# Reordering the second norm of a decoder layer: residual add, sums of squares, modulation groups and a larger ring of conditioning loads

## What is computed

```python
mod = jax.nn.silu(c) @ ada_w[l] + ada_b[l]
sh1, sc1, g1, sh2, sc2, g2 = jnp.split(mod[:, None, :], 6, axis=-1)
h = rms_norm(x) * (1.0 + sc1) + sh1
mix, ... = token_mixer(h, ...)          # ends with  merged @ w_out
x = x + g1 * mix
h = rms_norm(x) * (1.0 + sc2) + sh2
ff, s_cv = conv_ffn(h, ...)             # begins with  h @ w_up
x = x + g2 * ff
```

## Time and profile before

| what | value |
|---|---|
| three runs | 2243.47, 2246.07, 2248.70 us |
| median | 2246.07 us |
| profiled execution: span | 2245.0 us; its own time beside the span is not listed apart from the three runs |
| TensorE busy | 2200.8 us, 98% of the span |
| VectorE, ScalarE, GpSimd busy | 50%, 44%, 15% |
| DMA | 460.03 MB, mean 205 GB/s |
| granted TensorE clock, mean | 0.993 |

### The profile page before, as it was taken

How to read it: one execution, slowest core, us unless ns; L and a number is a source line. 1 busy time by engine, 2 the same in 40 slices (tenths; PEclk the granted TensorE clock), 3 DMA queues, 4 the chain that set the end, 5 groups by cost and what they waited for, 6 DMA issues and landing times. The chain is left out here.

```text
span 2245.0 us, 42389 instructions
## 1 busy us (share of the span) xinstructions
PE 2200.8 (98%) x17346; PEld 2073.4 (92%) x17346; DVE 1123.0 (50%) x1557; ACT 985.4 (44%) x1365; POOL 342.1 (15%) x529
## 2 busy tenths in 40 slices
PE   7999999999999999999999998999999999999998
PEld 3689999999999999999999987999999999999997
DVE  3346465564565444444445565555555555444443
ACT  3336463564454344454435334434434344333332
POOL 2000312322222221121202241000000000010000
PEclk9999999999999999999999999999999999999999
DMA  9987666666666767668666688555555555555553
GB/s 350 376 279 213 195 198 203 205 199 211 205 212 205 221 188 224 214 205 254 211 209 209 209 284 282 160 168 167 160 168 159 168 168 159 177 161 174 171 167 106
DMA packets 407411, 460.03 MB, mean 205 GB/s; under 512 B 14843, under 2 KB 379955, under 8 KB 406433
## 3 DMA queue, kind: packets, MB, share of 16 engines
q1 hardware_dynamic: 394192, 410.64, 57.2%
q0 software_dynamic: 12240, 46.03, 6.6%
q10 hardware_dynamic: 833, 1.26, 0.2%
HBM read 431.48 MB, written 26.39 MB: 204 GB/s over the span
## 5 line engine op out<-in xcount | busy, mean ns | idle before, releaser
L763 PE MATMUL ps<-xh,whi 128*128 128x288 f32 x3968 | 1195.1, 301 | 11.4 <-DVE xl L1745 5.0
L1688 DVE TENSOR_TENSOR wlo<-raw,whi 128x1024 fp32r<-128x1024 f32 x584 | 735.3, 1260 | 918.3 <-ACT whi L1255 916.0
L765 PE MATMUL ps<-xh,wlo 128*128 128x288 f32 x3968 | 1173.1, 296 | 0.0
L764 PE MATMUL ps<-xl,whi 128*128 128x288 f32 x3968 | 1172.0, 295 | 0.0
L1255 ACT ACTIVATE whi<-raw 128x1024 fp32r<-128x1024 f32 x584 | 616.6, 1057 | 764.5 <-PE ps L765 728.4
L763 PEld LDWEIGHTS ps<-xh,whi 128*128 128x128 f32 x3968 | 748.2, 189 | 53.4 <-issue 38.7
L764 PEld LDWEIGHTS ps<-xl,whi 128*128 128x128 f32 x3968 | 747.5, 188 | 0.0
L765 PEld LDWEIGHTS ps<-xh,wlo 128*128 128x128 f32 x3968 | 747.3, 188 | 0.0
L763 PE MATMUL ps<-ffh,whi 128*128 128x288 f32 x704 | 209.2, 297 | 0.0
L765 PE MATMUL ps<-ffh,wlo 128*128 128x288 f32 x704 | 208.4, 296 | 0.0
L764 PE MATMUL ps<-ffl,whi 128*128 128x288 f32 x704 | 208.3, 296 | 0.0
(11 more groups left out here) (422 smaller groups left out, 1646.8 us busy)
## 6 DMA issues: line engine op xcount, KB each, us to landing
raw<-in_w_in SPq DMA_DIRECT2D x288, 512.0 KB, 4.6
raw<-in_w_up SPq DMA_DIRECT2D x176, 512.0 KB, 3.5
raw<-in_w_down SPq DMA_DIRECT2D x88, 512.0 KB, 3.4
araw<-in_ada_w SPq DMA_DIRECT2D x74, 512.0 KB, 5.9
uraw_x<-in_ada_w SPq DMA_DIRECT2D x36, 512.0 KB, 10.0
raw<-in_w_out SPq DMA_DIRECT2D x32, 512.0 KB, 4.0
top<-in_ada_w SPq DMA_DIRECT2D x24, 512.0 KB, 8.0
afill<-in_ada_w SPq DMA_DIRECT2D x18, 512.0 KB, 8.5
```

The lines of the kernel that those rows point to most:

```text
L763: mm(o, whi[:, s, kk, cols], hi[:, kt0 + kk, :], start=first and kk == 0, stop=False)
L764: mm(o, whi[:, s, kk, cols], lo[:, kt0 + kk, :], start=False, stop=False)
L765: x = mm(o, wlo[:, s, kk, cols], hi[:, kt0 + kk, :], start=False, stop=last and kk == KC - 1)
L1688: TT(wlo[:, s], raw[:, s], whi[:, s].bitcast(F32), ALU.subtract).then_inc(lo_done, 1)
```

## The change

Six things change, all between w_out's first three quarters and w_up's first block:

- GpSimd adds x to `mixo` before P2 (eight adds in a row), so `second_part` on VectorE writes the finished x to `xT2`; the squares need VectorE alone. `sqacc` is made by two sums instead of a memset and three.
- The eight matmuls of the sums of squares stand ahead of `fill(2)`, `fill_turn(1)`, `fill(3)`, `fill(4)`. The last four tiles' squares are made two tiles at a time. Sixteen transposes without a use (`WARM`) go.
- The norm's groups are 2, 2, 4, 4, 4 tiles, and chunk u0 waits for its two halves apart.
- `wlo` of u0 and u1 is made after `second_part(7)`, that of u2 between the last two groups; P2 keeps five of its eight.
- The ring has 14 slots: ten as before and four in `merged`. Blocks 5, 6, 7 stand ahead of u1, u3, u5 (before: block 5 ahead of u0, 6 ahead of u1, 7 ahead of u3), and in P2 `fill(1)` stands ahead of `fill_turn(0)`.
- The order of loads follows that, and the spill waits for the third group (the same eight tiles).

```diff
-FRING = 10
+FILL_SLOTS = tuple(range(14)) + tuple(range(14)) + (0, 1, 10, 11)
 FILL_P2 = {4: 0, 6: 1}
-FILL_UP = {1: 6, 3: 7}
+FILL_UP = {1: 5, 3: 6, 5: 7}
+NORM2_GROUPS = ((0, 2), (2, 4), (4, 8), (8, 12), (12, 16))
...
             def fill_loads(a, b):
                 for e in range(a, b):
-                    if e >= FRING:
-                        sp.wait_ge(a_used, before_a(A_UP) + e - FRING + 1 + FREE)
+                    if fill_last(e) is not None:
+                        sp.wait_ge(a_used, before_a(A_UP) + fill_last(e) + 1 + FREE)
...
             fill_loads(4, 10)
-            first_up(0, 1, 2)
+            first_up(0, 1)
+            sp.wait_ge(xlo, XS + 5)
             fill_loads(10, 14)
+            first_up(2)
+            fill_loads(14, 18)
             first_up(3)
-            fill_loads(14, 24)
+            fill_loads(18, 24)
             first_up(4)
             fill_loads(24, 28)
             first_up(5)
...
             def p2_ahead(q):
+                if q in FILL_P2:
+                    fill(FILL_P2[q])
                 if q == 6:
                     fill_turn(0)
-                if q in FILL_P2:
-                    fill(FILL_P2[q])
             stream(N_P2, "s" * 8, length=1, kt0=12, halves=XS + 4, ahead_of=p2_ahead)
-            fill(2)
-            fill(3)
-            fill_turn(1)
-            pe.wait_ge(x1_acc, 3 + FREE)
+            pe.wait_ge(x1_acc, 2 + FREE)
             for t in range(8):
...
             x.then_inc(ms_done, 1)
+            fill(2)
+            fill_turn(1)
+            fill(3)
             fill(4)
-            pe.wait_ge(rs_done, 3)
-            fill(5)
-            for _ in range(WARM):
-                nc.tensor.transpose(R[:, 0, 0:P], ident[:, :], ident[:, :])
...
-            stream(up2_base(0), UP_KINDS, xparts=XS + 5, ahead_of=up_ahead)
+            stream(up2_base(0), UP_KINDS, xparts=XS + 6, halves=XS + 6, ahead_of=up_ahead)
...
+            for u in range(8):
+                if u < 5:
+                    lo(N_P2, u + LEAD)
+                second_part(u)
+                if u == 6:
+                    ada_block(A_UP, ab, ada_free, CN)
+            modulate(xT2, mixo, 3 * KT, 4 * KT)
...
             for u in range(8):
                 kt = slice(2 * u, 2 * u + 2)
-                pool.wait_ge(x1_p, 3 * (u + 1))
-                G(xT2[:, kt, :], xT2[:, kt, :], mixo[:, kt, :], ALU.add).then_inc(x1_a, 1)
...
+                pool.wait_ge(x1_m, u + 1)
+                pool.wait_ge(bank_free[u % 2], N_P1[1] + u // 2 + 1 + FREE)
+                G(mixo[:, kt, :], mixo[:, kt, :], xT2[:, kt, :], ALU.add).then_inc(x1_a, 1)
...
-            pool.wait_ge(x1_a, 8)
-            pool.wait_ge(xlo, XS + 7)
+            pool.wait_ge(x1_p, 24)
+            pool.wait_ge(xlo, XS + 8)
             pool.dma_start(x1_spill, xT2[:].rearrange("p a b -> p (a b)")).then_inc(spill_1, 16)
```

More of the change, by code:

```diff
@@ L51 @@
 XS = 5
-ZAB_Y = 4
+ZAB_Y = 3
 LEAD = 3
@@ L120, with fill_last, fill_count @@
 EXTRA = 3 * len(BY_FOUR)
-FRING = 10
+FILL_SLOTS = tuple(range(14)) + tuple(range(14)) + (0, 1, 10, 11)
 FILL_P2 = {4: 0, 6: 1}
-FILL_UP = {1: 6, 3: 7}
+FILL_UP = {1: 5, 3: 6, 5: 7}
+NORM2_GROUPS = ((0, 2), (2, 4), (4, 8), (8, 12), (12, 16))
+def fill_last(e):
+    return max([c for c in range(e) if FILL_SLOTS[c] == FILL_SLOTS[e]], default=None)
+def fill_count(e):
+    return FILL_SLOTS[:e + 1].count(FILL_SLOTS[e])
 def ahead(base, i, chunks, pairs):
@@ L177 @@
 EARLY_LOADS = 20
-WARM = 16
 def pieces_ahead(u, h):
@@ L852, in stream @@
                                 pe.wait_ge(bank_free[b % 2], N[1] + b // 2 + (PARTED // 2 - PARTED // 8) * start + FREE)
-                            if xparts is not None and b == 0:
+                            if xparts is not None and b == 0 and not (halves is not None and s == 0):
                                 pe.wait_ge(xlo, xparts + s + 1)
@@ L1287, in root, with modulate @@
                 A(rstd[:, :], lnms[:, :], ACT.Exp, scale=-0.5).then_inc(rs_done, 1)
-            def modulate(nth, tmp, shift, scale, groups=range(4)):
-                if nth == 2:
-                    act.wait_ge(sc_one, 1)
+            def modulate(tmp, shift, scale, groups):
                 for g in groups:
[L1294 to L1298, removed]
+                    act.wait_ge(ada_free, 2 * g + 2 + FREE)
+                    act.wait_ge(xn_done, g + 1)
+                    parts = 2 if g == 3 else 1
                     for t in range(4 * g, 4 * g + 4, 4 // parts):
@@ L1302, in modulate, with modulate_2 @@
                         x.then_inc(md_p, 1)
[L1303 to L1306, removed]
+                        act.wait_ge(md_p, t // 4 + 1 + (t == 14))
+                        act.wait_ge(md_s, 2 * (g + 1))
                         A(xh[:, t:t + 4 // parts, :], tmp[:, t:t + 4 // parts, :], ACT.Copy).then_inc(xhi, 1)
+            def modulate_2(tmp, shift, scale):
+                act.wait_ge(sc_one, 1)
+                for g, (a, b) in enumerate(NORM2_GROUPS):
+                    act.wait_ge(xn_done, 4 + g + 1)
+                    for kt in range(a, b):
+                        x = A(tmp[:, kt, 0:TP], tmp[:, kt, 0:TP], ACT.Identity, bias=mod[:, shift + kt, 0:1], scale=mod[:, scale + kt, 0:1])
+                    x.then_inc(md_p, 1)
+                    act.wait_ge(md_p, XS + g + 1)
+                    act.wait_ge(md_s, 2 * (4 + g + 1))
+                    if g == 0:
+                        act.wait_ge(used, N_UP[0] + FREE)
+                    A(xh[:, a:b, :], tmp[:, a:b, :], ACT.Copy).then_inc(xhi, 1)
             def unit(u):
@@ L1818, in _, with modulate, normal, sampled @@
                 early_chunk(n)
-            def modulate(nth, src, tmp, shift, scale):
+            def modulate(src, tmp, shift, scale):
+                def normal(g):
+                    a, b = NORM2_GROUPS[g]
+                    TT(tmp[:, a:b, :], src[:, a:b, :], mid(rstd[:, :], b - a), ALU.mult).then_inc(xn_done, 1)
+                def sampled(g):
+                    a, b = NORM2_GROUPS[g]
+                    dve.wait_ge(xn_done, 4 + g + 1)
+                    v = seq3(tmp[:, a:b, TP:T], LS)
+                    TT(v, v, rep3(mod[:, scale + a:scale + b, 1:NB], LS), ALU.mult).then_inc(md_s, 1)
+                    dve.wait_ge(md_s, 2 * (4 + g) + 1)
+                    TT(v, v, rep3(mod[:, shift + a:shift + b, 1:NB], LS), ALU.add).then_inc(md_s, 1)
+                def low(g):
+                    a, b = NORM2_GROUPS[g]
+                    dve.wait_ge(xhi, XS + 5 + g + 1)
+                    TT(xl[:, a:b, :], tmp[:, a:b, :], xh[:, a:b, :].bitcast(F32), ALU.subtract).then_inc(xlo, 1)
                 for p in range(2):
@@ L1826, in modulate @@
                 dve.wait_ge(sc_one, 1)
-                dve.wait_ge(rs_done, 2 * nth - 1)
+                lo(N_P2, 5 + LEAD)
+                lo(N_P2, 6 + LEAD)
+                dve.wait_ge(rs_done, 3)
                 nc.vector.reciprocal(rstd[:, :], lnms[:, :]).then_inc(rs_done, 1)
[L1829 to L1836, removed]
+                dve.wait_ge(rs_done, 4)
+                normal(0)
+                sampled(0)
+                normal(1)
+                sampled(1)
+                low(0)
+                normal(2)
+                low(1)
+                sampled(2)
+                normal(3)
+                sampled(3)
+                low(2)
+                ada_block(A_UP + 1, ab, ada_free, CN)
+                normal(4)
+                sampled(4)
+                low(3)
+                lo(N_P2, 7 + LEAD)
+                low(4)
             r = merged[0:MH]
```

60 lines of the change are left out of this document (31 added, 29 removed).

## The result

The changed kernel takes 2258.05 us (median of six runs, 2255.79 to 2258.88) against 2246.65 for the kernel before (six runs, 2242.72 to 2252.08): a ratio of 1.0047 [1.0037, 1.0057]. It is **slower by about 11 us**, outside the forecast's range of 2240 to 2250.5.

The account below looks back on a forecast made before the run. The DMA engines were taken to bound the stretch, with u6's load landing unchanged. A 2.07 us gain at u5 less 1.8 for the clock gave -0.3 us from 2246.07, so 2245.8 us, range 2240 to 2250.5.

Parts of the forecast that it names:

- The step that failed: GpSimd's eight adds, 11.3 us alone and 19.2 at the longest (8 x 2.40), are hidden under P2's 26 us.
- The cover: Without P2 hiding the adds, P2 would end up to a few us later, which the loads below would hide again.
- the forecast's sum: Path from u6's landing at 1382.3 through turn 3, u4, block 7 and turn 4 to u5 at 1390.60.
- the bounds of 0 and 3.62: Clock loss for u4 and block 7: nothing if the clock holds, 3.62 us if both run at 1.2 GHz.
- the 1.8 taken: Clock loss after TensorE's longer wait ahead of u4, taken as the middle of the bounds: 1.8 us.
- u0 10.4 us earlier than before: The shorter norm chain lets u0 start near 1355 instead of 1366.05: 11 us gained at this point.
- u6's load at 70.1: The same 35 loads and the spill stand ahead of u6, so it lands at 1382.3 again.
- a gain of 2.07 in order: At u5, before any clock loss: start at 1390.60 instead of 1392.67, a gain of 2.07 us.
- The spill costs the loads: The spill of x, 2304 KB in GpSimd's queue, delays the loads by 5.8 us, now those of blocks 6, 7 and u5.
- Turn 3 behind `wlo` of u6: Turn 3, ahead of u4, needs a bias VectorE adds only after `wlo` of u6, so it comes at 1384.68.
- The first: Rival: the spill delays no loads, u6 lands 5.8 us earlier, gain 7.9, time 2238.2 us; chance 0.20.
- The second: Rival: ring slots hold SyncE's loads if block 6 begins after about 1376; 4.7 us slower, 2250.8 us; chance 0.11.

Follow-up runs that it names:

- experiment 1: Changed kernel with one more wait on GpSimd, so that at most two adds run ahead of `second_part`: 2250.02 us, 1.0015 of the kernel before.
- experiment 4: Changed kernel with the spill of x issued when all eight blocks are done, instead of with the third group: 2255.25 us, 1.0041 of the kernel before.
- experiment 5: Changed kernel with both the paced adds of experiment 1 and the late spill of experiment 4: 2244.7 us, 0.9990 of the kernel before.
- experiment 6: experiment 1 plus, in w_up's first block, rows copied ahead of `whi` and bias added ahead of `wlo`: 2243.64 us, 0.9983 of the kernel before.
- experiment 7: Changed kernel with paced adds, late spill, and rows and bias first (experiment 4 and experiment 6 together): 2237.7 us, 0.9957 of the kernel before.
- experiment 8: Kernel before, without the change, plus late spill and rows and bias first: 2245.02 us, 0.9995 of the kernel before.
- experiment 3: Changed kernel with GpSimd's fifth add waiting for `wlo` of w3, splitting the eight adds into two fours: 2249.77 us, 1.0018 of the kernel before.
- experiment 2: Kernel before with only the eight adds moved ahead of P2 and what must follow them: 2252.47 us, 1.0028 of the kernel before.

## Why the prediction was wrong

**The step that failed** is what the forecast said of the eight adds on GpSimd: "They are hidden: P2's eight chunks take 8 x 3.26 = 26 us, and each `second_part` needs only its own add", with its bound of 8 x 2.40. The bound priced GpSimd's side of the collision, and that side cost nothing: the adds took 10.97 us, 1.37 each. VectorE's side was not priced at all. The forecast went by the adds of the kernel before, of which four met `wlo` and paid (2.27 to 2.40 us instead of 1.41 to 1.43), so it looked as if GpSimd were the one that pays. The same trace held the other case three times, which the forecast did not use; the first of them:

```profile
1323.24 2.67 POOL L2395 TENSOR_TENSOR sqacc<-sqacc,mixo 128x1152 f32<-128x1152 f32 x1 [1.33 <-issue]
...
1324.09 2.91 DVE L1688 TENSOR_TENSOR wlo<-raw,whi 128x1024 fp32r<-128x1024 f32 x1 [3.69 <-ACT whi L1255]
```

Beside one of GpSimd's sums of squares, begun 0.85 us earlier, `wlo` takes 2.91 us instead of 1.22 and ends 1.09 us after the sum: it was VectorE that waited. In the row of eight adds it paid 11.1 us in one instruction. The Trainium skill, "SBUF — State Buffer", section "Who interferes with whom", says that a VectorE instruction with two inputs in SBUF contends with a GpSimd instruction that reads SBUF. For VectorE's two-port modes that section adds that whoever issues first has the shared port pair for the whole instruction. The traces agree on who contends, and go further than one instruction: 12.35 us beside eight adds, each of 1.37.

**The cover was wrong as well.** The forecast said that a late P2 would be hidden by the loads below. The issue of those loads hung on the very instruction that was late: w7's load needs the slot that `wlo` of w3 frees, and the queue is in order. The forecast took the wait for the last state's output to be what starts the loads in both kernels; in the changed one they start 6.2 us later from the mark (14.35 against 8.15). u6 then came 7.5 later. From `whi` of u6 to u5 the changed kernel takes 11.49 us (1391.48 to 1402.97), where the forecast's sum has 8.32 at the full clock: 3.2 more, nearly all of it the clock (0.67 granted from 1390 to 1400), within the bounds of 0 and 3.62 but above the 1.8 taken. So u5 came 7.5 - 2.07 + 3.2 = 8.6 later, u15 9.9, and the time was 11.4 longer; the last 1.5, of which 0.4 lies outside the span, is not traced.

That the loads carry the loss, and not P2's own delay, is read from the trace; no run delays the loads alone. With P2 late by 8.4 us at w2, u0 still began 3.2 us earlier than before, and ahead of u3 and u4 TensorE's waits end with a load or with what stands behind one.

**What held.** With the run of adds broken up (experiment 1), the other steps came out:

- u0 10.4 us earlier than before; forecast 11.
- u6's load at 70.1 from the mark against 69.8; forecast the same time.
- u5 0.1 us later; forecast 0.3 earlier, after a gain of 2.07 in order and a loss of 1.8 to the clock. The loss comes out at 1.8 here; as the middle between two bounds that is luck, and in the changed kernel it was 3.2.
- The spill costs the loads 5.7 to 6.0 us wherever it is issued ahead of them; forecast 5.8.
- Turn 3 behind `wlo` of u6: it ended TensorE's wait in the changed kernel and in experiments 1, 4 and 5, and went when the order was changed (experiment 6).

**The rivals.** The first (the spill slips in without delaying the loads) falls with experiments 4 and 5. The second (the larger ring blocks the queue) did show its wait, 6.0 us of SyncE for block 6, but the DMA's slices have no hole after it (355 to 344 GB/s in the slices from 1380 to 1392 us, and more while SyncE waited), and experiment 1, with the same ring, loads on time: it did not decide. Block 6 did begin late, 63.9 us from the mark, which is 1376.4 on the forecast's clock and so at the edge that it gave, but the loads were late as well. The sign that it forecast, slower, came by another mechanism: this rival named GpSimd's adds beside VectorE only as a way to lose the norm chain's gain, not as a hold on the loads.

## What to carry to other kernels

When work is moved to GpSimd so as to run ahead of its need, ask which VectorE instructions with two SBUF inputs fall into its run, and what hangs on each of them, loads above all: a run without pauses can cost such an instruction its whole length, and a wait every second instruction gave back 8 of 11 us here. A gain off the bound arrives only when what stands behind it is moved as well: here the shorter norm chain was worth nothing with paced adds alone (experiment 1), and with a later spill and small copies put ahead of work that waits for a load the kernel was 7 us faster than with those two edits and no change (experiments 7 and 8). Before a delay is called hidden by a later transfer, check that it does not hold back the issue of that transfer.

## What the runs showed of the hardware

- A subtraction of two SBUF tiles on VectorE can be kept waiting by a whole unbroken run of GpSimd adds, not only by the one in progress: the run, plus 1.23 us, plus 0.15 to 0.17, for runs of 2.83, 5.55 and 10.97 us. Its row begins 0.30 to 0.31 us ahead of the run's first add in all three; in experiment 1 another `wlo`, 0.25 us ahead of an add, took its usual 1.22 us and the add 2.26. So the start of a row does not tell which of the two will wait. In experiment 3's second run of four it got in after one add; why, stays open.
- `second_part`'s instructions with an input from PSUM were not held up: in experiment 2 the first two ran inside the eight adds in their usual time (0.88 us), and only the one behind them with two SBUF inputs stood still.
